# A two-layer decoder step on one NeuronCore: SyncE's loads wait for their own memory instead of a stage fence, and VectorE takes no value columns while it ranks the decode rows

## What is computed

```python
def peer_ffn(h, w_q, sub_keys, u_tab, v_tab):            # per token row x of rmsnorm(h)
    q = (x @ w_q).reshape(blk, P_HEADS, P_QDIM)
    s1 = einsum('nhd,hkd->nhk', q[..., :half], sub_keys[:, 0]); s2 = ...   # 128 scores each
    v1, i1 = lax.top_k(s1, 16); v2, i2 = lax.top_k(s2, 16)
    vals, ci = lax.top_k((v1[..., :, None] + v2[..., None, :]).reshape(...), 16)
    expert = take(i1, ci // 16) * 128 + take(i2, ci % 16); gate = softmax(vals)
    act = gelu(einsum('nd,nhkd->nhk', x, u_tab[expert]))
    return einsum('nhk,nhkd->nd', gate * act, v_tab[expert])

h = rmsnorm(x, norm_mix[1]);  q, cmp, sel, win, gate = nsa_project(h, pos, nsa_w_in)  # 2608 columns
o = g0 * o_cmp + g1 * o_sel + g2 * o_win;   x = x + o @ nsa_w_out
x = x + peer_ffn(rmsnorm(x, norm_ffn[1]), peer_w_q[1], peer_sub_keys[1], peer_u[1], peer_v[1])
```

## Time and profile before

| | before |
|---|---|
| median of 3 runs (lowest, highest) | 2637.49 us (2624.43, 2644.32) |
| profiled execution; its span | 2624.34 us; 2622.6 us |
| busy PE, DVE, POOL, ACT | 1959.6, 1462.1, 1389.9, 721.4 us |
| moved in the span; mean rate | 806.19 MB; 307 GB/s |
| of it the gathers' queue; SP's queue | 673.82 MB; 130.89 MB |
| value columns on PE (358 slots); folds on DVE (218 slots) | 766.3 us; 280.6 us |
| mean granted TensorE clock | 0.857 of 2.4 GHz |

### The profile page before, as it was taken

The page is one execution under the profiler, slowest core; times in us unless marked ns, Lnnn a source line. Parts: engine busy times, 40 slices in busy tenths (PEclk is TensorE's granted clock), DMA queues, the critical chain, the costliest instruction groups (busy, mean ns, idle before and its releaser), DMA issues. The chain is left out here.

```text
span 2622.6 us, 23237 instructions
## 1 busy us (share of the span) xinstructions
PE 1959.6 (75%) x7254; PEld 1008.9 (38%) x7254; DVE 1462.1 (56%) x3293; ACT 721.4 (28%) x1716; POOL 1389.9 (53%) x1415
## 2 busy tenths in 40 slices
PE   5979798688988767986857889676677777748346
PEld 4446467244444324545412345352122323227111
DVE  1024346576465623674954268666366777763864
ACT  1111112366675402431211135111132333310001
POOL 2021016667677734674774356658465555443774
PEclk9975699798999887897979889788898999965579
DMA  7141509887999998899889989997989999896797
GB/s 222 65 160 44 177 1 335 311 306 283 383 408 411 406 385 294 325 351 403 321 326 400 307 328 347 386 335 255 390 335 360 358 358 372 296 349 232 275 392 305
DMA packets 253891, 806.19 MB, mean 307 GB/s; under 512 B 41813, under 2 KB 46425, under 8 KB 244249
## 3 DMA queue, kind: packets, MB, share of 16 engines
q0 software_dynamic: 176496, 673.82, 68.1%
q1 hardware_dynamic: 77128, 130.89, 14.1%
q10 hardware_dynamic: 144, 0.00, 0.0%
HBM read 798.90 MB, written 14.04 MB: 310 GB/s over the span
## 5 line engine op out<-in xcount | busy, mean ns | idle before, releaser
L3142 PE MATMUL g_acc<-g_vrow,g_diag 128*128 128x512 f32 (+1 forms) x1432 | 766.3, 670 | 260.2 <-ACT g_diag L3120 128.5
L3013 POOL DMA_INDIRECT g_vrow<-in_peer_v_dram,f_idx x576 | 598.2, 1039 | 458.1 <-PE g_acc L3142 161.6
L2997 POOL DMA_INDIRECT f_u<-in_peer_u_dram,f_idx x576 | 579.1, 1005 | 375.3 <-DVE g_dot L3078 244.3
L3078 DVE CUSTOM_DVE_ANT_0 f_u<-f_u,g_h_ps 128x1024 f32<-128x1024 f32 x576 | 685.1, 1214 | 116.8 <-DMA f_u<-in_peer_u_dram,f_idx 66.2
L3142 PEld LDWEIGHTS g_acc<-g_vrow,g_diag 128*128 128x128 f32 (+1 forms) x1432 | 262.9, 198 | 659.4 <-issue 460.4
L3055 DVE SCALAR_TENSOR_TENSOR x<-g_vrow,g_w,x 128x1024 f32<-128x1024 f32 x218 | 280.6, 1287 | 22.1 <-DMA g_vrow<-in_peer_v_dram,f_idx 11.6
L1068 ACT ACTIVATE g_slab<-g_side 64x256 f32<-64x256 f32 x512 | 193.8, 378 | 116.9 <-PE g_side L1019 110.8
L3039 DVE TENSOR_TENSOR g_w<-g_gelu,f_gate 128x4 f32<-128x4 f32 x144 | 26.3, 183 | 357.3 <-ACT g_gelu L3110 356.8
L1030 PE MATMUL g_side<-g_slab 128*128 128x512 f32 x256 | 144.2, 646 | 50.1 <-ACT g_slab L1068 50.0
L3120 ACT ACTIVATE g_diag<-const,g_w 128x128 f32<-128x128 f32 (+1 forms) x358 | 126.0, 381 | 195.8 <-DVE g_w L3039 194.4
L1170 PE MATMUL g_side<-g_slab 128*128 128x512 f32 (+3 forms) x288 | 129.6, 593 | 60.2 <-DMA g_slab<-in_nsa_w_in_dram 60.2
(11 more groups left out here) (402 smaller groups left out, 2407.8 us busy)
## 6 DMA issues: line engine op xcount, KB each, us to landing
g_slab<-in_nsa_w_in_dram SPq DMA_DIRECT2D x15, 2048.0 KB, 18.9
g_slab<-in_peer_w_q_dram SPq DMA_DIRECT2D x14, 2048.0 KB, 19.8
mp_w<-in_mlstm_w_in_dram SPq DMA_DIRECT2D x6, 2048.0 KB, 10.6
g_slab<-in_nsa_w_out_dram SPq DMA_DIRECT2D x6, 2048.0 KB, 14.4
f_u<-in_peer_u_dram,f_idx POOLq DMA_INDIRECT x576, 7.5
g_vrow<-in_peer_v_dram,f_idx POOLq DMA_INDIRECT x576, 7.5
g_slab<-in_state_win_kv_dram SPq DMA_DIRECT2D x8, 1024.0 KB, 8.9
out_win_s_dram<-in_state_win_kv_dram SPq DMA_DIRECT2D x1, 8128.0 KB
```

The source lines that it names most:

```text
L2997: pool.indirect_dma_start(u[:, i % RU, :], None, u_table, bass.IndirectOffsetOnAxis(ap=idx[:, col:col + 1], axis=0), element_offset=layer ...
L3013: pool.indirect_dma_start(vrow[:, i % RV, :], None, v_table, bass.IndirectOffsetOnAxis(ap=idx[:, col:col + 1], axis=0), element_offset=lay ...
L3078: dve.tensor_tensor_reduce(row, row, h_ps[:], 1.0, 0.0, ALU.mult, ALU.add, dot[:, g % 2, k:k + 1]).then_inc(dotted, 1)
L3142: mm = pe.matmul(acc[0:n, a, :], diag[:, q % (2 * GRP), 0:n], vrow[:, i % RV, a * 512:a * 512 + 512], start=first and on_pe[i] == on_pe[GR ...
```

## The change

It has four parts. In `prompt.sync` the fence goes. For tile 0 the gain vector waits until POOL has placed layer 0's last ranking, into memory that the ranking used, and weight piece 0 until the last cached row has been turned (`rows_turned`). For tile 1 gain and pieces 0 and 1 wait for the last matmul of `route` (`w_used` 12) and its last scores. `decode.sync` waits for `w_used` 24 instead of the fence. The gain and sub-keys of `route` move ahead of its first two weight pieces, to the end of `prompt.sync`. And `SHARES` gets two entries: no folds from beat 1110, two in four from 1200 instead of three.

```diff
@@ Projection
-        self.gain = [place(11264, [P, D]), place(14848, [P, D])]
+        self.gain = [place(16004, [P, D]), place(11264, [P, D]), place(0, [P, D])]
...
-        yield from S.norm_dve(dve, at, step, beat, 2 * t + 3, t, self.gain[s])
+        yield from S.norm_dve(dve, at, step, beat, 2 * t + 3, t, self.gain[t])
...
-    def sync(self, sp, t):
-        S, s, n = self.S, t // 2, TILES[t][1]
-        sp.dma_start(self.gain[s][0:n], S.I["norm_mix"][1].partition_broadcast(n)).then_inc(S.gain_in, 16)
+    def sync(self, sp, t, rows_turned=None):
+        S, n = self.S, TILES[t][1]
+        sp.dma_start(self.gain[t][0:n], S.I["norm_mix"][1].partition_broadcast(n)).then_inc(S.gain_in, 16)
         for j in range(2):
+            if t == 0 and j == 0:
+                sp.wait_ge(rows_turned, CSTR * DEC_B)
             self.load(sp, t, j)
@@ PromptWork.sync
-        sp.wait_ge(S.fence, 3 * (2 + 2 * t))
         if t == 0:
             sp.dma_start(proj.b_gate[:], ...).then_inc(proj.b_gate_in, 16)
+            sp.wait_ge(ranks.placed, LAYER0_RANKS)
         else:
             sp.wait_ge(proj.saved, 16 * 3)
-        proj.sync(sp, t)
+            sp.wait_ge(S.w_used, 12)
+            sp.wait_ge(route.scored, NJ)
+        proj.sync(sp, t, rows_turned)
...
             sp.dma_start(proj.ring[0][:, a], w_out[:, :, a * WB:(a + 1) * WB]).then_inc(S.w_in[a], 16)
+        sp.wait_ge(proj.turned, 3 * t + 1)
+        sp.dma_start(route.gain, I["norm_ffn"][1].partition_broadcast(P)).then_inc(S.gain_in, 16)
+        if t == 0:
+            sp.wait_ge(self.stored, 8)
+            sp.dma_start(route.keys, ...).then_inc(route.keys_in, 16)
@@ RouteWork.sync
-        sp.wait_ge(S.fence, 3 * (3 + 2 * t))
-        sp.dma_start(self.gain, I["norm_ffn"][1].partition_broadcast(P)).then_inc(S.gain_in, 16)
-        if t == 0:
-            sp.dma_start(self.keys, ...).then_inc(self.keys_in, 16)
@@ DecodeWork.sync
-        sp.wait_ge(S.fence, 18)
         sp.wait_ge(proj.saved, 16 * 6)
+        sp.wait_ge(S.w_used, 24)
         proj.sync(sp, 2)
@@
 SHARES = ((0, (3,)), (160, (1, 3)), (300, (3,)), (379, (1, 3)), (470, ()), (556, (1, 3)), (742, ()), (802, (3,)),
-          (918, (1, 2, 3)))
+          (918, (1, 2, 3)), (1110, ()), (1200, (1, 3)))
```

More of the change, by code:

```diff
@@ L1709, in dve, with sync @@
         S.leave(dve, self.o_added, 2 * t + 2)
-    def sync(self, sp, t):
+    def sync(self, sp, t, ranks, route, rows_turned):
         S, proj, n = self.S, self.proj, 8 * (t + 1)
         I = S.I
-        sp.wait_ge(S.fence, 3 * (2 + 2 * t))
         if t == 0:
             sp.dma_start(proj.b_gate[:], I["nsa_b_gate"][0].partition_broadcast(P)).then_inc(proj.b_gate_in, 16)
+            sp.wait_ge(ranks.placed, LAYER0_RANKS)
         else:
             sp.wait_ge(proj.saved, 16 * 3)
-        proj.sync(sp, t)
+            sp.wait_ge(S.w_used, 12)
+            sp.wait_ge(route.scored, NJ)
+        proj.sync(sp, t, rows_turned)
         for c in range(2):
@@ L1743, in sync @@
             sp.dma_start(proj.ring[0][:, a], w_out[:, :, a * WB:(a + 1) * WB]).then_inc(S.w_in[a], 16)
+        sp.wait_ge(proj.turned, 3 * t + 1)
+        sp.dma_start(route.gain, I["norm_ffn"][1].partition_broadcast(P)).then_inc(S.gain_in, 16)
+        if t == 0:
+            sp.wait_ge(self.stored, 8)
+            sp.dma_start(route.keys, I["peer_sub_keys"][1].rearrange("h s k d -> k (h s) d")).then_inc(route.keys_in, 16)
 class Ranks:
@@ L2004, in sync @@
             sp.dma_start(self.proj.ring[0][:, j], w_q[:, :, j * WB:(j + 1) * WB]).then_inc(S.w_in[j], 16)
-        sp.wait_ge(S.fence, 3 * (3 + 2 * t))
-        sp.dma_start(self.gain, I["norm_ffn"][1].partition_broadcast(P)).then_inc(S.gain_in, 16)
-        if t == 0:
-            sp.dma_start(self.keys, I["peer_sub_keys"][1].rearrange("h s k d -> k (h s) d")).then_inc(self.keys_in, 16)
         for j in range(2, NJ):
@@ L2933, in sync @@
         for t in range(2):
-            self.prompt.sync(sp, t)
+            self.prompt.sync(sp, t, self.ranks, self.route, self.cached.turned)
             self.route.sync(sp, t)
```

## The result

Twenty runs of each kernel: before 2637.06 us median, changed 2612.18 (2591.50 to 2630.76). The ratio is 0.9914, with a 95% interval of 0.9894 to 0.9934: 23 us less, 17 to 28. The forecast was 2593, 44 less. So the sign and the range (2555 to 2630) held, the size was about half of the forecast, and of the three cases the one with the chance of 0.25 came: within 1% of before. The profiled execution took 2606.30 us, with a span of 2604.5.

The account below looks back on a forecast made before the run. No engine's total decides: transfers are full in some stretches and have room in others. Terms -3 - 12 - 7 + 2 - 11 - 8 - 5.5 = -44.5 us, giving 2593 against the median 2637.49; range 2555 to 2630.

Parts of the forecast that it names:

- the three cases: Whole kernel: faster, under 2611 us, chance 0.67; within 1% of before, 0.25; slower, over 2664, 0.08.
- Routes: Route of tiles 0 and 1: early gain (and tile 0's keys) removes DVE's gain waits, -12 and -11 us.
- rival 3: Route: w_q pieces come late and take 8 us of each gain wait's term; 2609 us, chance 0.12.
- Borders: Three projection borders: earlier weight requests cut PE's waits, -3, -7 and -8 us; +2 for transfers during tile 0's ranking.
- A fifth of the 11.5: Second border: share of PE's longest wait, at a later piece, counted as gained within the -7 us.
- a little for later pieces: Decode's border: gain beyond the first two pieces' 6.6 us, as later pieces are requested when the first are used; within -8.
- Prefetch in the ranking: Ranking of tile 0: 4.7 MB more pass there and may make the dots' rows late, +2 us, ends 0 and +7.
- Table: End of decode: 30 slots' folds leave DVE and become PE columns, -5.5 us, ends -20 and +28.
- +0.5 for five columns among the scores: Decode's scores: five columns cost 17.5 us, less 3.4 each for faster matmuls at the upper clock behind them.
- Rival 2: End of decode: eleven columns lengthen PE's path, +24 us; 2661 us with borders giving nothing; scores over 60 us; chance 0.07.
- rival 1: Whole kernel: transfers are full and only bytes count, so each term is at its small end; -18.6, 2619 us, chance 0.17.
- Rival 4: Decode's scores: columns hold PE's clock at the upper level, scores 51 us become about 25; total 2578 us, chance 0.10.

Follow-up runs that it names:

- route alone: Kernel before with only route's gain vector and sub-keys asked for early, projection weights and SHARES as before: ratio 0.9945, -14.5 us.
- 48 columns apart with and without early requests: Changed kernel, 48 gate columns in their own memory instead of a ring slot: 2585.78 us; same with first projection weights behind the fence again: 2604.30 us.
- table alone: Kernel before with only the new SHARES table, thirty slots from VectorE to TensorE, all loads as before: ratio 1.0003, +1 us.

## Why the prediction was right in sign and too large

- **Routes (-12 and -11, measured -14.5 together).** The step that failed is the middle that was taken between the ends. The lower ends, -7 and -8, were the ones in which the stretch must end as full as before, and 15 is what came. The reason given for more (the rings may end emptier, since the next stretches refill them) did not hold in tile 0's window: the transfers stayed full through the stall, the rings filled in it, and a removed stall gives only what they could not take in. That the third piece would be late next was right, but only by 3 us for both routes (8.15 and 8.88 in the changed kernel, 8.38 and 8.84 in the route alone, 5.71 and 8.34 before), not by rival 3's 8 each: rival 3 is out.
- **Borders (-3, -7 + 2, -8, measured -3).** The step "the first two pieces' waits go" was right, and what it was worth was wrong. A ring of two asks for the third piece when the first is used. Only the wait for the first moves that moment; the wait for the second turns up again at the third. "A fifth of the 11.5" and "a little for later pieces" had no mechanism behind them. And the longest waits of the first two borders, 15.5 and 11.5, were for the fifth piece, whose request hung on a slot that 48 columns held: that was to be read from the list of pieces and the issues on SP, and was not. (At decode's border the longest, 5.7, was for the second piece, as the prediction counted it.)
- **Prefetch in the ranking (+2).** The stretch 1245 to 1290 is at 1.03 now and its DVE less busy, 38.21 against 44.47; with the borders at -3 in all the term cannot be told apart.
- **Table (-5.5, measured +1).** Ranking and tail gained as said, by about 12 us in the profile. The step that failed is +0.5 for five columns among the scores, taken from one column's 3.4 us. The score stretch was 52, 63, 64 and 66 us in the four profiles with this table (changed kernel, 48 columns apart with and without early requests, table alone). Rival 2's condition, over 60 us, was there in three of them; the gain behind it kept the sum at nothing.
- **Sum.** What came, 23 us less (17 to 28), lies between the forecast and rival 1 (-18.6), and the interval holds rival 1. The total fell into the range because that reached past rival 1, not because the forecast's terms were right. Rival 1's numbers for route, border and table are close to what was measured, but its reason is only half right: at the borders bytes were not the limit, or the fifth piece could not have given 29 us.
- **The signs named ahead.** The gain waits and the waits for the first pieces went, and DVE ranks without folds. The third w_q piece was to wait no longer than now and waits 3 us longer, both routes together. The score stretch of the changed kernel's profile, 52 us at a mean clock of 0.69, is as foretold; that it was this profile is luck, as the three others show. And of what the prediction named as making it wrong, the dots' waits for `f_u` came right behind the gain, as the last sentence of the prediction has it; PE and DVE waited there for value rows too.

The rule of the Trainium skill that was weighed, 358 GB/s for one core's reads ("DMA: Bandwidth & Descriptors", Specifications), is contradicted once more: the changed kernel moved 404 GB/s over 95 us. Rival 4 leaned on the Trainium skill's sentence that throttled is the default state and activity releases it ("TensorE: Matmul & The Clock Gate", What's actually happening). With the table alone the trace does not bear this out: PE was busy all of 65.60 us at a mean granted clock of 0.52. What makes a column bring the upper level at one time and not at another is open; no run here separated it.

## What to carry to other kernels

Removing a wait on a load in a ring is worth only what it moves the next request: follow the requests on the queue, each back to the use that freed its slot, before a wait is counted as gain, and look for a small piece that holds a whole slot. A stall during which other queues fill their buffers costs only what those buffers could not take in, so its length is an upper bound on the gain, and the work that went on is to be taken off it. Two edits at one border need not be a sum: in the profiles the early request took 6 us off the waits alone and 27 beside the free slot. And where the same instructions take 52 us in one execution and 66 in another, a term that rests on one profile's clock has no single size.

## What the runs showed of the hardware

- While SP's queue and the gathers' queue both had work, they shared the full engines nearly packet for packet: 1242 packets to 1239 in the 18 us shown above, and 701 to 698 in the changed kernel from 1180 to 1190 us. The gathers' packets were larger (4.51 MB / 1242 = 3.6 KB against 2.2 KB), so they had 62% of the bytes and SP 38%. By that a 2 MB piece needs an estimated 14 us beside gathers; the projection pieces took 18.9 us from issue to landing at the median in both kernels.
- The same 256 thin matmuls and five columns took 52 or 66 us in two profiles, with a mean granted clock of 0.69 or 0.52 and PE without a pause in both. Behind two of these columns (3.76 and 3.66 us) the thin matmuls ran at the upper level in the changed kernel's profile, 32 in 3.8 us; behind the same two (3.76 each) they ran at the half level with the table alone, 32 in 6.88 us.
